# Second attention on one Trainium2 core: output copies per head pair, norm over two steps, turns at other places

## The reference

```
k, v = shared_kv(x, ...)                       # kv = rms_norm(x) @ kv_w; k is normed per 64 columns
q = rms_norm_2((h @ w_q).reshape(...), q_norm)
lam = exp(sum(lq1 * lk1)) - exp(sum(lq2 * lk2)) + lam_init
s = einsum("bqhcd,bkhcd->bhcqk", qc, k) * scale + bias     # bias: table over distance buckets
pm = softmax(where(rel <= 0, s, NEG_INF_2))
attn = pm[:, :, 0] - lam * pm[:, :, 1]
o = einsum("bhqk,bkhe->bqhe", attn, v)                     # 128 columns per head
o = rms_norm_2(o, subln) * (1.0 - lam_init)
return o.reshape(...) @ w_o
```

## Time and profile before

| | us |
|---|---|
| median of 3 runs | 2107.18 (2101.96 to 2107.51) |
| the profiled execution | 2104.71 |
| its span | 2102.9 |
| mean granted clock of PE | 0.974 |
| first group product of the second attention | 1326.1 |
| scores of step 0 | 1441.82 |
| scores of step 8 / 12 / 20 / 28 | 1480.56 / 1512.76 / 1562.45 / 1604.55 |
| last product with v | 1631.89 |
| last output product | 1656.8 |

### The profile page before, as it was taken

The page is one execution under the profiler, slowest core; times in us unless marked ns, Lnnn a source line. Parts: engine busy times, 40 slices in busy tenths (PEclk is TensorE's granted clock), DMA queues, the critical chain, the costliest instruction groups (busy, mean ns, idle before and its releaser), DMA issues.

```text
span 2102.9 us, 26554 instructions
## 1 busy us (share of the span) xinstructions
PE 1988.4 (95%) x9640; PEld 1615.3 (77%) x9640; DVE 1220.0 (58%) x1727; ACT 852.2 (41%) x1343; POOL 442.8 (21%) x609
## 2 busy tenths in 40 slices
PE   8999999999999888999999989798777999999988
PEld 8998678888887777877877868686666777878877
DVE  5445465555455994477466456734556666465555
ACT  4323342222235884344244235534665444243333
POOL 3110039998815451100000001100000200000010
PEclk9999899999999999999999999899899999999999
DMA  4221023264442332222323223221111123223232
GB/s 153 84 79 65 21 90 107 85 213 157 167 167 88 121 128 83 87 82 94 105 84 107 81 91 110 92 91 45 51 51 36 61 90 104 87 90 110 80 104 97
DMA packets 65077, 201.64 MB, mean 96 GB/s; under 512 B 6422, under 2 KB 19222, under 8 KB 63948
## 3 DMA queue, kind: packets, MB, share of 16 engines
q1 hardware_dynamic: 57372, 166.39, 23.6%
q0 software_dynamic: 7600, 33.84, 4.5%
HBM read 184.44 MB, written 15.77 MB: 95 GB/s over the span
## 4 chain that ended last, share of the span: by engine, by line
PE 84%; DVE 8%; ACT 5%; issue 2%; DMA 1%; POOL 1%; SPq 0%; ACTq 0%; DVEq 0%; POOLq 0%
PE ps L449 60%; PE ps L587 7%; PE ps L1729 5%; PE ps L738 2%; PE ps L1843 1%; PE ps L438 1%; PE ps L813 1%; DVE w_lo L428 1%; ACT w_hi L424 1%; ACT t L2033 1%; PE ps L1957 1%; DMA cp<-mix_cp 1%; POOL t L529 1%; DMA raw<-in_wstream 1%; PE ps L769 0%
## 5 line engine op out<-in xcount | busy, mean ns | idle before, releaser
L428 DVE TENSOR_TENSOR w_lo<-raw,w_hi 128x1024 fp32r<-128x1024 f32 x308 | 396.7, 1291 | 169.0 <-ACT w_hi L424 168.5
L449 PE MATMUL ps<-x_hi,w_hi 128*128 128x512 f32 x1152 | 458.8, 398 | 3.9 <-DVE w_lo L428 2.6
L449 PE MATMUL ps<-x_lo,w_hi 128*128 128x512 f32 x1152 | 455.7, 396 | 0.0
L449 PE MATMUL ps<-x_hi,w_lo 128*128 128x512 f32 x1152 | 453.5, 394 | 0.0
L424 ACT ACTIVATE w_hi<-raw 128x1024 fp32r<-128x1024 f32 x308 | 322.1, 1049 | 247.5 <-DMA raw<-in_wstream 154.2
L449 PE MATMUL ps<-a_hi,w_hi 128*128 128x512 f32 x704 | 279.8, 397 | 7.7 <-DVE pp L1584 4.8
L449 PE MATMUL ps<-a_hi,w_lo 128*128 128x512 f32 x704 | 279.8, 397 | 0.0
L449 PE MATMUL ps<-a_lo,w_hi 128*128 128x512 f32 x704 | 279.6, 397 | 0.0
L529 POOL TENSOR_TENSOR t<-t,sq 128x512 f32<-128x512 f32 x49 | 72.6, 1483 | 938.4 <-ACT sq L520 936.4
L449 PEld LDWEIGHTS ps<-x_hi,w_hi 128*128 128x128 f32 x1152 | 216.4, 188 | 69.0 <-issue 11.4
L449 PEld LDWEIGHTS ps<-x_hi,w_lo 128*128 128x128 f32 x1152 | 216.7, 188 | 49.8
(11 more groups left out here) (402 smaller groups left out, 3043.0 us busy)
## 6 DMA issues: line engine op xcount, KB each, us to landing
raw<-in_wstream SPq DMA_DIRECT2D x308, 512.0 KB, 3.3
ev<-mix_ev POOLq DMA_DIRECT2D x8, 1024.0 KB, 5.0
mix_cp<-c_p POOLq DMA_DIRECT2D x8, 640.0 KB, 3.4
cp<-mix_cp POOLq DMA_DIRECT2D x8, 640.0 KB, 6.3
mix_ev<-v_b POOLq DMA_DIRECT2D x8, 512.0 KB, 3.5
fall<-fall POOLq DMA_DIRECT2D x4, 544.0 KB, 4.9
h<-in_xT SPq DMA_DIRECT2D x4, 528.0 KB, 6.2
mix_ev<-e_r POOLq DMA_DIRECT2D x1, 2048.0 KB, 9.4
```

The source lines that it names most:

```text
L428: e.tensor_tensor(w_lo[:, u.slot, :], raw[:, u.c % 2, :], w_hi[:, u.slot, :], ALU.subtract)\
L449: last = e.matmul(ps[:, bank, :], wt[:, u.slot, w], x[:, k0 + k, 0:SEQ], start=(k == 0 and n == 0), stop=(k == kt - 1 and n == 2))
```

## The change

- The table's two products follow group 1, not group 0, and DVE's copies with lambda's rest too.
- The k turn of pair 0 goes through bank 6 and no longer waits for the q turn's low part.
- The four products with v of a pair write four parts of bank 6. DVE copies them once (`dve_hold(p)`), ACT squares them once into `sq[:, 1]`, after its exponentials; a new reduction on DVE (`dve_out_sum`) makes the four sums. Products with v wait for the copy only at a pair's start.
- `dve_out` is in two parts: sums in step i % 4 == 3, reciprocal and scaling in the next.
- Turns: on PE all at the step's end, q and k in the same steps as before, o one step later; on ACT and DVE each one step after PE's.
- Fills: group 5 at steps 10 to 13 and 15 to 18 (before 9, 10, 12, 13, 14, 16, 17, 18), output at 22, 23, 24, 26, 27, 29, 31, 33 (before 21, 22, 23, 25, 26, 28, 30, 32). One step more.

```diff
-    for k, i in enumerate((9, 10, 12, 13, 14, 16, 17, 18)):
+    for k, i in enumerate((10, 11, 12, 13, 15, 16, 17, 18)):
         FILL[i] = ("group", 5, k)
-    for k, i in enumerate((21, 22, 23, 25, 26, 28, 30, 32)):
+    for k, i in enumerate((22, 23, 24, 26, 27, 29, 31, 33)):
         FILL[i] = ("out", k // 2, k % 2)
...
+    def turn_bank(kind, p):
+        return 6 if (kind, p) == ("k", 0) else 7
+
     def turn_pe(e, kind, p):
-        k = TURN[kind, p]
+        k, b = TURN[kind, p], turn_bank(kind, p)
         if k == 0:
             e.wait_ge(tab_ok, 2)
-        ge(e, tr_ev, k)
+        if b == 7:
+            ge(e, tr_ev, k)
...
                 if g == 0:
                     e.wait_ge(lam_v, 1)
                     e.matmul(ps[:, 7, 0:2], ones[:, :], small[:, 0, 0:2], start=True, stop=True).then_inc(lam_mm, 1)
+                if g == 1:
                     e.wait_ge(lam_a, 1)
                     e.wait_ge(tab_in, 16)
                     e.matmul(ps[0:8, 6, :], rel[:, :], onehot[:, 0:SEQ], start=True, stop=True)
...
         def pe_pv(g):
             p, qt, N = step(g)
             e.wait_ge(pt_ok, g + 1)
-            ge(e, od_ok, g)
+            if g % 4 == 0:
+                ge(e, od_ok, p)
...
-                last = e.matmul(ps[:, 6, 0:P], PT2[g % 2][:, j * P:(j + 1) * P], v_tok[:, j, p * P:(p + 1) * P],
+                last = e.matmul(ps[:, 6, qt * P:(qt + 1) * P], PT2[g % 2][:, j * P:(j + 1) * P], v_tok[:, j, p * P:(p + 1) * P],
...
-        def dve_hold(g):
-            p, qt, N = step(g)
-            e.wait_ge(pv_mm, g + 1)
-            if g % 4 == 0 and p >= 2:
+        def dve_hold(p):
+            e.wait_ge(pv_mm, 4 * p + 4)
+            if p >= 2:
                 e.wait_ge(tr_mm, TURN["o", p - 2] + 1)
-            e.tensor_copy(o_held(p)[:, qt, :], ps[:, 6, 0:P]).then_inc(od_ok, 1)
-
-        def dve_out(p):
+            e.tensor_copy(o_held(p).rearrange("p q c -> p (q c)"), ps[:, 6, :]).then_inc(od_ok, 1)
+
+        def dve_out_sum(p):
             r = slice(4 * p, 4 * p + 4)
-            e.wait_ge(os_ok, 4 * p + 4)
             n = dve.did(e.scalar_tensor_tensor(small[:, 0, 0:4], state[:, 15, r], eps_o[:, 0:1], state[:, 15, r],
                                                ALU.mult, ALU.mult))
+            e.wait_ge(os_ok, p + 1)
+            e.reduce_sum(state[:, 12, r], sq[:, 1, 0:SEQ].rearrange("p (q c) -> p q c", q=4), AX_X).then_inc(oa_ok, 1)
+            e.wait_ge(oa_ok, p + 1)
             e.wait_ge(dve_did, n)
             e.scalar_tensor_tensor(state[:, 13, r], state[:, 12, r], 1.0 / (P * (1.0 - LAM) ** 2), small[:, 0, 0:4],
                                    ALU.mult, ALU.add).then_inc(ov_ok, 1)
+
+        def dve_out(p):
+            r = slice(4 * p, 4 * p + 4)
             e.wait_ge(or_ok, p + 1)
...
-        def act_square(g):
...
+        def act_square(p):
+            e.wait_ge(od_ok, p + 1)
+            e.wait_ge(qn_s, 14 if p == 0 else 16)
+            ge(e, oa_ok, p)
+            e.activation(sq[:, 1, 0:SEQ], o_held(p).rearrange("p q c -> p (q c)"), ACT.Square).then_inc(os_ok, 1)
...
-        for i in range(37):
+        for i in range(38):
             if who == "pe":
                 if i < 32:
                     pe_scores(i)
-                if i < 28 and i % 4 in (1, 2):
-                    turn_pe(e, "qk"[i % 4 - 1], i // 4 + 1)
...
                 if 3 <= i < 35:
                     pe_pv(i - 3)
-                if i % 4 == 3 and 7 <= i < 35:
-                    turn_pe(e, "o", (i - 7) // 4)
+                if i < 28 and i % 4 in (1, 2):
+                    turn_pe(e, "qk"[i % 4 - 1], i // 4 + 1)
+                if i % 4 == 0 and 8 <= i < 35:
+                    turn_pe(e, "o", (i - 8) // 4)
             elif who == "act":
-                if 4 <= i < 36:
-                    act_square(i - 4)
                 if i < 32:
                     act_exp(i)
+                if i % 4 == 3 and i >= 7:
+                    act_square((i - 7) // 4)
...
```

More of the change, by code:

```diff
@@ L158, in build @@
         pt2b = sb("pt2b", [P, SEQ], F32, c)
-        o_junk = sb("o_junk", [P, P], F32, c)
     pw_up = sb("pw_up", [P, 3, 32, 5])
@@ L342, in build @@
     oy_ok = sem("oy_ok")
+    oa_ok = sem("oa_ok")
     wo_mm = sem("wo_mm")
@@ L1661, in build @@
             TURNS.append(("k", i // 4 + 1))
-        if i % 4 == 3 and i >= 7:
-            TURNS.append(("o", (i - 7) // 4))
+        if i % 4 == 0 and i >= 8:
+            TURNS.append(("o", (i - 8) // 4))
     TURNS.append(("o", 7))
@@ L1749, in group_act @@
             ge(e, qn_s, k - 1)
+            if g == 4 and tb >= 2:
+                e.wait_ge(oa_ok, 1)
             ins = e.activation(sq[:, k % 2, 0:SEQ], src, ACT.Square, scale=r)
@@ L1782, in turn_pe @@
             for qt in range(4):
-                last = e.matmul(ps[:, 7, qt * P:(qt + 1) * P], o_held(p)[:, qt, :], flip[:, :], start=True, stop=True)
+                last = e.matmul(ps[:, b, qt * P:(qt + 1) * P], o_held(p)[:, qt, :], flip[:, :], start=True, stop=True)
         else:
@@ L1787, in turn_pe @@
             for tb in range(4):
-                last = e.transpose(ps[:, 7, tb * P:(tb + 1) * P], group_store(g, tb)[:, (p % 4) * P:(p % 4 + 1) * P],
+                last = e.transpose(ps[:, b, tb * P:(tb + 1) * P], group_store(g, tb)[:, (p % 4) * P:(p % 4 + 1) * P],
                                    ident[:, :])
@@ L1798, in turn_at @@
         if kind == "k":
-            return kr_hi[:, p % 2, :], kr_lo[:, p % 2, :], ps[:, 7, :], vec("k_norm")
+            return kr_hi[:, p % 2, :], kr_lo[:, p % 2, :], ps[:, turn_bank(kind, p), :], vec("k_norm")
         hi, lo = (o0_hi, o0_lo) if p < 4 else (o1_hi, o1_lo)
@@ L1828, in out2_pe @@
                 e.wait_ge(pt_ok, 32)
-                e.wait_ge(od_ok, 32)
+                e.wait_ge(od_ok, 8)
             elif j == 7 and h == 0:
@@ L1917, in attention2_first @@
                     head_scales_dve(e, g)
-                if g == 0:
+                if g == 1:
                     e.wait_ge(tab_mm, 1)
@@ L1971, in pe_pv @@
             e.wait_ge(pt_ok, g + 1)
-            ge(e, od_ok, g)
+            if g % 4 == 0:
+                ge(e, od_ok, p)
+            if g == 0:
+                e.wait_ge(tr_ev, TURN["k", 0] + 1)
             if g % 16 == 0:
@@ L2023, in dve_out @@
             e.wait_ge(dve_did, n)
-            e.wait_ge(od_ok, 4 * p + 4)
             o = o_held(p)
@@ L2040, in act_turn @@
             e.activation(PT2[g % 2][:, 0:N], ps[:, 5, 0:N], ACT.Copy).then_inc(pt_ok, 1)
-        def act_square(g):
-            p, qt, N = step(g)
-            e.wait_ge(od_ok, g + 1)
-            ge(e, os_ok, g)
-            e.activation(o_junk[:, :], o_held(p)[:, qt, :], ACT.Square, accum_out=col(12, g)).then_inc(os_ok, 1)
+        def act_square(p):
[3 more added lines that the diff above has]
+            e.activation(sq[:, 1, 0:SEQ], o_held(p).rearrange("p q c -> p (q c)"), ACT.Square).then_inc(os_ok, 1)
         def act_root(p):
@@ L2053, in turns @@
         def turns(i, turn):
-            if i % 4 == 1 and i < 28:
+            if i % 4 == 2 and i < 28:
                 turn(e, "q", i // 4 + 1)
-            if i % 4 == 2 and i < 28:
+            if i % 4 == 3 and i < 28:
                 turn(e, "k", i // 4 + 1)
-            if i % 4 == 0 and i >= 8:
-                turn(e, "o", (i - 8) // 4)
-        for i in range(37):
+            if i % 4 == 1 and i >= 9:
+                turn(e, "o", (i - 9) // 4)
+        for i in range(38):
             fill, done = FILL.get(i), FILL.get(i - 1)
@@ L2095, in attention2 @@
             else:
-                if 4 <= i < 36:
-                    dve_hold(i - 4)
+                if i % 4 == 3 and i >= 7:
+                    dve_hold((i - 7) // 4)
                 if i < 32:
@@ L2102, in attention2 @@
                 if i % 4 == 3 and i >= 7:
-                    dve_out((i - 7) // 4)
+                    dve_out_sum((i - 7) // 4)
+                if i % 4 == 0 and i >= 8:
+                    dve_out((i - 8) // 4)
                 turns(i, turn_dve)
```

## The result

The changed kernel takes 2088.73 us (median of 6 runs, 2084.83 to 2096.73) against 2107.13 for the kernel before: a ratio of 0.9921, 95% interval 0.9902 to 0.9941. (The ratio is made from all executions and stands for 16.6 us; the two medians are 18.4 apart.) A second series gave 2088.82 against 2103.98 beside it, 15.2 us less, ratio 0.9925 (0.9910 to 0.9940). All ratios here are of fast executions: two of the kernel before (5644.52 and 3323.18 us) and one of experiment 4 (3898.45) ran slow and are left out. The forecast was 2090, in a range of 2078 to 2100.

A forecast was written before the change was run, and what follows sets the result against it. PE, busy 1988.4 of 2102.9 us, was taken as the bound, so only its waits count. Term 1 (8.75), term 2 (4.1) and Term 3 (2.3) sum to 15.2 us less: 2104.7 becomes 2089.5, rounded to 2090; range 2078 to 2100.

The forecast's parts named there:

- Term 1: Ahead of the loop: table products behind group 1 remove PE's pause after the lambda product; 8.75 us less.
- term 2: Ahead of the loop: k of pair 0 in bank 6 no longer waits for q's low part; 4.1 us less.
- The rule that I used: On PE: after a pause of 2.3 us or more, products follow at 1.2 GHz, costing 1.65 us more.
- Term 3: In the loop: old waits and slow stretches go, new ones come; 2.3 us less, 8 us both ways.
- The new waits: In the loop: PE's waits for low parts and links made in the same step, 35.0 us in all.
- the slow stretches: In the loop: lower clock behind pauses; seven go (11.6 us) and four come (6.6 us).
- The waits of a product for the copy of the step before: In the loop: 5.8 us of PE waits go, as the copy is asked for once in four steps.
- The place that I chose as the main cost: Last step of a pair: k's turn stands behind the root on ACT and delays the next scores; 12.2 us.
- The waits for evictions that were to go: Group halves of steps 9 and 14 move later, so 5.6 and 2.8 us of PE waits go.
- output turns hardly wait: Sign of being right, in the loop: output turns, which waited 6.6 + 6.3 us before, hardly wait.
- It moves up whole: The rest of the program: same work behind a PE that sets the pace, so it only starts earlier.
- The rule of the Trainium skill: ACT's table switch: about 1.38 us of drain on top of each load, 9.7 us over seven steps; not counted.

The follow-up runs named there:

- experiment 4: The changed kernel with the table and the first k turn's bank as before, so only the loop's changes; 2103.22 us, ratio 0.9992 to the kernel before.
- Run 8: The changed kernel with 32 copies of 128 columns out of one part of bank 6 instead of 8 merged copies; 2088.16 us, ratio 0.9910.
- run 6: The changed kernel with all fills (group 5 and output) at the steps of the kernel before; 2100.33 us, ratio 0.9984.
- run 9: The changed kernel with k's turn ahead of the root on ACT and ahead of the four sums on DVE; 2088.91 us, ratio 0.9926.
- run 10: On top of run 9, PE makes the q and k turns behind the scores of the next step; 2083.22 us, ratio 0.9897.
- run 11: On top of run 10, the output turn is also made behind the scores; 2071.73 us, ratio 0.9842.
- run 1: The kernel before with only the table's products moved behind group 1; 2097.87 us, ratio 0.9975.
- run 3: The kernel before with both edits ahead of the loop, table and bank; 2096.61 us, ratio 0.9954.
- run 7: The changed kernel with only the output fills at their old steps, group 5's at the new ones; 2092.09 us, ratio 0.9939.
- run 12: On top of run 11, ACT evicts the last v tiles ahead of k's turn and the root in step 19; 2073.55 us, ratio 0.9855.
- run 2: The kernel before with only the first k turn moved to bank 6; 2105.06 us, ratio 1.0006.

## Why the prediction was right, and where it was not

**Term 1 and term 2** were right, in mechanism and size: 8.3 and 4.0 for 8.75 and 4.1, and 12.3 to 12.6 together. The table's products cost the 1.2 that I took between 1.1 and 2.2. What I left out is that a stage that is shorter can hand a lower clock to the next one: in the three kernels with these edits and the old loop, B was 1.7 to 4.0 longer, at nearly the same idle time (40.9 to 41.3 after 40.8), by one profile each. The rule that I used, that products follow at the lower clock after a pause of 2.3 us or more, failed already in the kernel before: its first scores stand behind 2.65 us and ran at a clock of 1.00.

**Term 3** came out as forecast (2.3; measured 2.0 and 1.9), for reasons that were partly wrong and that cancel, so that agreement is luck. With table and bank as before the same loop made B 4.5 shorter (run 4). In detail:
- The new waits were forecast at 35.0 and the slow stretches at 5.0 less than before. The trace has idle time 5.2 less, where my working made it 2.7 more, and busy time 3.2 more. By the list of waits the new ones are 27.9 (o 8.2, k 7.2, q 2.8, output turns 7.0, copies of the transposes 1.9, the v tiles 0.8 more than before). Each link was near and a little shorter: 1.7, 3.7, 0.9 and 0.9 us ahead of scores 8, 12, 24 and 28, where I had 2.3, 4.3, 1.4 and 1.4, and none at 16; 2.8 in step 9, where I had 4.9 with its evictions; 2.7, 2.6 and 2.8 in steps 14, 21 and 25, where I had about 3. The clock was not to be had by a fixed price per pause.
- "The waits of a product for the copy of the step before, 5.8, which is asked for once in four steps now": this step failed. Run 8 asks in every step again and waits 1.5. These waits went mostly with the fills, since run 6 brings 3.7 of them back with merged copies. The prices of the work itself held: copy 0.68 and reduction 0.69 us, square 0.62, where I had 0.65, 0.69 and 0.615.
- "The place that I chose as the main cost", k's turn behind the root, exists and behaves as described (run 9 and step 7), but it is not the main cost: without it the idle time is 2.5 less and the total is the same.
- The waits for evictions that were to go (5.6 and 2.8) are gone. Both halves moved by one step, not by "two steps or one".
- That "output turns hardly wait" did not come true: 12.9 became 7.0. The working had it right, with 2.0 and 3.1 in steps 20 and 28 (measured 2.0 and 2.6) and more at the end, and the sign contradicted it.
- Not seen at all: the place of a turn relative to the scores. Run 9's edit and the moves of runs 10 and 11 together gain 17 us, with no work removed; run 9 alone gained nothing in the total. My reading is that a turn at a step's end holds back the scores behind it, and these start the next step's work on DVE and ACT, so the chain pays the wait again. Of the 17.4 us between run 9 and run 11 in stage B, 6.5 are idle time, which this reading can account for; the other 10.9 are clock.

**The sum.** "It moves up whole", said of the rest of the program, put at nothing what cost 1.5 us (447.2 after 445.7). By the profiles the change is worth 12.6 + 2.0 - 1.5 = 13.1 us, where the forecast had 15.2; the medians of the two series differ by 18.4 and 15.2. The code ahead of stage A is the same in all kernels and took 1321.6 to 1331.5 us in their profiles, so that the median came within 1.3 us of 2090 is in part luck.

**The rule of the Trainium skill.** In the changed kernel too the root starts at 1473.62, 0.01 us after its table load of 1.28 us ends. The load itself starts 0.02 us after ACT's copy ahead of it ends (1472.33 after 1472.31). No drain of 1.38 us stands on the path, so the Trainium skill's page "ScalarE: Activation LUTs" (section "What ACT_TABLE_LOAD costs") overprices the switch here, and the sum was right to go by the row.

**Left open.** Table and bank (0.46%) and the loop (0.08%) sum to 0.54%, the whole is 0.75 to 0.79%. The intervals, some 0.15 to 0.2% on each, allow for the difference. By the stages of the profiles the parts do add up: 9.7 us for table and bank (12.3 of A, less 2.5 that B and 0.1 that the rest gave back), 3.0 for the loop (0.1 + 4.5 - 1.6), against 13.1 for the whole. What decides the clock behind a pause stays open; no run here shows it.

## What to carry to other kernels

In a loop of in-order queues, ask of every instruction that may wait what stands behind it on its own engine: put it behind whatever starts the other engines' next work. Of the gain of the change, taking two pauses out ahead of the loop carried more than half (0.46 of 0.75 to 0.79%). In the loop the fills decided: with group 5's halves at their old steps the new order lost, and fewer, larger copies on an engine that is not waited for showed no gain. Judge such edits by the stage's idle and busy time apart, and by many executions: stage B took 215.4 to 219.4 us in four kernels with the same loop code.

## What was not expected of the hardware

A pause of PE of 2.6 us was followed by full clock in one kernel (3.9 us for the step behind it) and by the 1.2 GHz level in another (6.9 us), with the same products and the same wait. In the kernel before, in the changed one, in its repetition and in runs 4, 6 and 10 the first step took 3.8 to 3.9 us; in runs 1, 3, 7, 8, 9, 11 and 12 it took 5.4 to 5.5, with the bank alone 6.8. So the prediction's fixed price of 1.65 us per pause stands for cases from 0 to 2.9.

The same happened once more far behind the change. 351 us behind the end of stage B, after the same pause of 2.5 us in code that no edit touched, the next 4 us ran at a clock of 1.00 in the kernel before and in runs 1, 2, 3 and 8, and at 0.57 to 0.67 in the changed kernel and all the others, 1.5 us longer. An edit in one place moved the price of a pause in another. PE left that pause 350.9 to 351.3 us behind the end of stage B in all of them, so its own timing on the way there does not tell the cases apart.
